# Attention in one kernel: the weights of a step are turned ahead of the next scores and copied ahead of the next exponential

## What is computed

```python
blocks = [(0, 16)] + [(s, min(s + 128, L)) for s in range(16, L, 128)]
for s, e in blocks:
    sc = einsum('bqhd,bkhd->bhqk', q[:, s:e], k[:, :e]) * 96 ** -0.5
    mask = arange(e)[None, :] <= arange(s, e)[:, None]
    p = softmax(where(mask, sc, -inf))
    outs.append(einsum('bhqk,bkhd->bqhd', p, v[:, :e]))
o = concatenate(outs, axis=1).reshape(bsz, L, 1024)
return o @ w_out
```

## Time and profile before

| | |
|---|---|
| median of 3 runs | 2978.79 us (2968.76 to 2986.44) |
| profiled execution | 2991.16 us, span 2989.3 |
| TensorE matmul busy | 2820.3 us, 94% of the span |
| TensorE weight load busy | 2387.6 us, 80% |
| VectorE, ScalarE, POOL busy | 1126.5, 1073.3, 968.6 us (38, 36, 32%) |
| mean granted TensorE clock | 0.942 |
| chain that ended last | PE 88%, DVE 6%, ACT 3%, issue 2% |
| HBM traffic | 211.24 MB read, 71 GB/s over the span |

### The profile page before, as it was taken

One profiled execution on the slowest core, in us unless ns is written; L12 is line 12 of the kernel. 1 busy time (PEld: TensorE's weight loads), 2 busy tenths in 40 slices (PEclk: granted clock), 3 DMA queues, 4 the chain that ended last, 5 costly groups with the idle time before them and its releaser, 6 DMA issues.

```text
span 2989.3 us, 38670 instructions
## 1 busy us (share of the span) xinstructions
PE 2820.3 (94%) x16552; PEld 2387.6 (80%) x16552; DVE 1126.5 (38%) x1571; ACT 1073.3 (36%) x1574; POOL 968.6 (32%) x413
## 2 busy tenths in 40 slices
PE   6999999799999978999999989999889999899999
PEld 4777778577777866777777989999857767699999
DVE  5333331433333166665555131112344344421111
ACT  3333332333333334544544232233343333333222
POOL 3343434334343431222222434443320000343442
PEclk9999999899999989999999999999986678899999
DMA  3232323123232211111111222222210000122222
GB/s 117 87 109 87 109 87 99 51 94 102 94 102 94 92 49 32 55 57 50 43 43 43 92 71 86 93 91 92 68 49 8 15 15 8 57 92 93 85 92 85
DMA packets 61289, 215.82 MB, mean 72 GB/s; under 512 B 8128, under 2 KB 8512, under 8 KB 61120
## 3 DMA queue, kind: packets, MB, share of 16 engines
q1 hardware_dynamic: 55440, 199.78, 20.3%
q10 hardware_dynamic: 5680, 13.58, 1.4%
HBM read 211.24 MB, written 2.10 MB: 71 GB/s over the span
## 4 chain that ended last, share of the span: by engine, by line
PE 88%; DVE 6%; ACT 3%; issue 2%; ACTq 0%; POOL 0%
PE psum L363 71%; PE psum L584 4%; PE psum L814 1%; PE psum L780 1%; PE psum L453 1%; PE psum L443 1%; PE psum L752 1%; PE psum L565 1%; DVE sb_square L1350 1%; PE psum L756 1%; PE psum L778 1%; PE psum L816 1%; DVE sb_scaled L1350 1%; PE psum L797 1%; PE psum L460 0%
## 5 line engine op out<-in xcount | busy, mean ns | idle before, releaser
L315 POOL TENSOR_TENSOR sb_w_lo<-sb_w_raw,sb_w_hi 128x1024 fp32r<-128x1024 f32 x377 | 916.3, 2434 | 1881.1 <-ACT sb_w_hi L941 1881.0
L363 PE MATMUL psum<-sb_h_hi,sb_w_hi 128*128 128x264 f32 (+1 forms) x2904 | 818.8, 334 | 65.7 <-DVE sb_h_lo L1354 51.3
L363 PE MATMUL psum<-sb_h_lo,sb_w_hi 128*128 128x264 f32 (+1 forms) x2904 | 800.1, 328 | 0.0
L363 PE MATMUL psum<-sb_h_hi,sb_w_lo 128*128 128x264 f32 (+1 forms) x2904 | 796.2, 326 | 0.0
L941 ACT ACTIVATE sb_w_hi<-sb_w_raw 128x1024 fp32r<-128x1024 f32 x377 | 395.1, 1053 | 567.4 <-PE psum L363 475.7
L363 PEld LDWEIGHTS psum<-sb_h_hi,sb_w_hi 128*128 128x128 f32 x2904 | 491.4, 190 | 129.9 <-issue 55.2
L363 PEld LDWEIGHTS psum<-sb_h_lo,sb_w_hi 128*128 128x128 f32 x2904 | 490.6, 190 | 47.2 <-issue 3.6
L363 PEld LDWEIGHTS psum<-sb_h_hi,sb_w_lo 128*128 128x128 f32 x2904 | 490.2, 191 | 44.9
L363 PE MATMUL psum<-sb_mix_hi,sb_w_hi 128*128 128x264 f32 (+1 forms) x1680 | 422.4, 315 | 6.9 <-DVE sb_mix_lo L1840 5.1
L363 PE MATMUL psum<-sb_mix_lo,sb_w_hi 128*128 128x264 f32 (+1 forms) x1680 | 420.2, 314 | 0.0
L363 PE MATMUL psum<-sb_mix_hi,sb_w_lo 128*128 128x264 f32 (+1 forms) x1680 | 418.8, 313 | 0.0
(11 more groups left out here) (235 smaller groups left out, 2643.3 us busy)
## 6 DMA issues: line engine op xcount, KB each, us to landing
sb_w_raw<-in_weights SPq DMA_DIRECT2D x377, 512.0 KB, 3.3
sb_decay<-in_decay ACTq DMA_DIRECT2D x16, 640.0 KB, 3.9
sb_resid<-in_x ACTq DMA_DIRECT2D x1, 2048.0 KB, 11.8
out<-sb_resid SPq DMA_DIRECT2D x8, 256.0 KB, 2.0
sb_table<-in_rope_table ACTq DMA_DIRECT2D x1, 264.0 KB, 2.6
sb_s<-in_positions ACTq DMA_DIRECT2D x1, 256.0 KB, 5.7
sb_cols<-in_cols ACTq DMA_DIRECT2D x1, 158.5 KB, 7.1
sb_resid<-in_meta ACTq DMA_DIRECT2D x1, 64.0 KB, 11.8
```

What stands on the lines that cost most here:

```text
L315: e.tensor_tensor(g.w_lo[:, u % 4, :], g.w_raw[:, u % 2, :], g.w_hi[:, u % 4, :].bitcast(F32), ALU.subtract).then_inc(S["w_lo"], 1)
L363: mm = e.matmul(g.psum[0:m, at + b, 0:wd], w[:, slot, P * i:P * i + m], xs[:, tile, c:c + wd], start=first and n == 0, stop=last and n == 2)
```

## The change

In each iteration of the loop, TensorE turns the weights of step i - 2 and multiplies those of step i - 3 by V ahead of the scores of step i; before, it turned those of i - 1 and multiplied those of i - 2 behind them. ScalarE copies the turned weights of step i - 2 ahead of the exponential of step i; before, it copied those of i - 1 behind it. The calls of `dve_finish` move from n = 1 and 5 to n = 2 and 6. Behind the loop stand the calls that the shift leaves over.

```diff
--- before.py
+++ after.py
@@ -873,11 +873,11 @@
     pe_pair_keys(g, e, 1)
     for i in range(ALL_STEPS):
         pair, n = divmod(i, NS)
+        if i >= 2:
+            pe_turn_p(g, e, i - 2)
+        if i >= 3:
+            pe_times_v(g, e, i - 3)
         pe_scores(g, e, i)
-        if i >= 1:
-            pe_turn_p(g, e, i - 1)
-        if i >= 2:
-            pe_times_v(g, e, i - 2)
         if pair + 1 < PAIRS:
             if n == 1:
                 pe_pair_totals(g, e, pair + 1, 0)
@@ -893,6 +893,8 @@
                 pe_pair_keys(g, e, pair + 2)
         for m, tiles in FILL.get(i, ()):
             pe_mla_out(g, e, m, tiles)
+    pe_turn_p(g, e, ALL_STEPS - 2)
+    pe_times_v(g, e, ALL_STEPS - 3)
     pe_turn_p(g, e, ALL_STEPS - 1)
     pe_times_v(g, e, ALL_STEPS - 2)
     pe_times_v(g, e, ALL_STEPS - 1)
@@ -1252,9 +1254,9 @@
     act_pair_keys(g, e, 1)
     for i in range(ALL_STEPS):
         pair, n = divmod(i, NS)
+        if i >= 2:
+            act_copy_pt(g, e, i - 2)
         act_exp(g, e, i)
-        if i:
-            act_copy_pt(g, e, i - 1)
         if pair and pair + 1 < PAIRS:
             if n == 0:
                 act_pair_keys(g, e, pair + 1)
@@ -1266,6 +1268,7 @@
             act_pair_out(g, e, pair - 1)
         if pair + 2 < PAIRS and n == 7:
             act_pair_q_squares(g, e, pair + 2)
+    act_copy_pt(g, e, ALL_STEPS - 2)
     act_copy_pt(g, e, ALL_STEPS - 1)
     act_pair_out(g, e, PAIRS - 1)
 
@@ -1854,9 +1857,9 @@
     for i in range(ALL_STEPS):
         pair, n = divmod(i, NS)
         dve_top(g, e, i)
-        if n == 1 and pair:
+        if n == 2 and pair:
             dve_finish(g, e, pair - 1, 1)
-        if n == 5:
+        if n == 6:
             dve_finish(g, e, pair, 0)
         if n == 6 and pair:
             dve_pair_out(g, e, pair - 1)
```

## The result

The changed kernel took 3024.80 us in the median of 4 runs (3024.39 to 3032.16), the kernel before 2980.34 beside it: a ratio of 1.0143, 95% interval 1.0122 to 1.0164. It is slower by 1.4%, 42.5 us. The forecast was 3009, its range 2986 to 3035. The profiled execution took 3024.94 (span 3023.1), 33.8 us more than that of before, for which the sum had said 30.1. That of before, 2991.16, is 11 us above its median, so the two profiles show less of a difference than the medians.

A forecast was written before the change was run, and what follows sets the result against it. TensorE's own stream was taken as the bound. Terms of 5.5, 0.1, 14.4 and 10.1 us, with 0 for the clock, sum to 30.1, giving 3009 us on the median 2978.8; own range 3000 to 3020, outer range 2986 to 3035.

The forecast's parts named there:

- a move of the extras: Extra work ending an iteration (totals, output turn, queries, keys; ScalarE's extras) goes ahead of turning and copy.
- n = 3 to 4: Scores of step n = 4 wait for a copy now behind both root halves: +2.05 us, 7 times, 14.4 us.
- n = 7 to 1: Scores of n = 0 wait for a copy behind query squares, 5.5 us; totals ahead of turning at n = 1, +0.1.
- rival A: Longer gaps keep the clock down, early returns in pairs 5 and 6 lost, falls come earlier: +54, 3033 us; chance 0.2.
- n = 6: Second queries wait for the previous output's low part, now also behind a finish on VectorE: 2.16 us idle, sum +10.1 us.
- The clock, taken as 0 net: Granted clock in the loop: later returns before n = 4 against earlier ones at n = 5, taken as 0 net.
- B: Denser blocks bring the clock's early return in pairs 0 to 4 too: -28, net +2, 2981 us; chance 0.11.
- C: Totals directly behind the scores of n = 1 keep the clock up: 38 us faster, 2941 us; chance 0.07.
- B2: The copy gets by the root, so no loss ahead of n = 4's scores: +16, 2995 us; chance 0.09.
- D: The change does what its words say and TensorE's listed waits go with nothing in exchange: 2960 us; chance 0.03.

The follow-up runs named there:

- experiment 1: Kernel before with only the TensorE and VectorE part of the change, ScalarE's order as before: 3006.3 us, ratio 1.0094.
- experiment 2: Kernel before with only ScalarE's new order, TensorE and VectorE as before: 3018.7 us, ratio 1.0126.
- Experiment 3: Changed kernel with ScalarE's copy at n = 3 put back ahead of the two halves of the reciprocal root: 3004.8 us, ratio 1.0085.
- experiment 9: Kernel of experiment 7; at n = 5 first queries ahead of turning and times V, exponential ahead of copy, finish behind last Newton step: 2962.1 us, ratio 0.9933.
- experiment 7: Kernel before with ScalarE's copy ahead of the exponential in every iteration and the keys at n = 7 instead of 6: 2970.2 us, ratio 0.9962.
- experiment 8: Changed kernel with the root at n = 3 and the squares at n = 7 back behind ScalarE's copy: 3015.4 us, ratio 1.0106.
- experiment 12: Kernel of experiment 8 with the output's low part on VectorE run at n = 5 instead of n = 6: 2967.6 us, ratio 0.9950.
- experiment 10: Kernel of experiment 7 with query squares ahead of copy and exponential at n = 7, and low part ahead of n = 6's maximum: 2946.3 us, ratio 0.9886.

## Why the prediction was right, and where its sizes were off

- **That the change is a move of the extras, not of the turning,** carried the direction. TensorE's and ScalarE's rows of the kernel after show it, and experiments 1 and 2 show each half to cost by itself.
- **n = 3 to 4:** forecast +14.4, measured +15.2 on that step, with 2.0 us ahead of the scores each time. Experiment 3 took it away alone, and the profiled loop lost 12 us with it. Shown.
- **n = 7 to 1:** forecast +5.6 over the steps 7-0, 0-1 and 1-2; measured +13.8. The squares cost their 0.9 us a time and the maximum came earlier, as worked out. But the gap of 0.9 to 1.0 us that was to stand ahead of the totals isn't there in pairs 1 to 6. In pair 3 the second product (2363.61 + 1.29) and the squared keys (2364.20 + 0.61) came when expected, and the scores of n = 1, which at the clock of before would have ended at about 2364.1, ended at 2365.57. The lower clock filled the gap with slower work. Over these steps idle time fell by 0.6 us and the busy time of the same work grew by 14.3: rival A's mechanism, which had been priced at 13.
- **n = 6:** the gap was forecast at 2.16 us and measured at 2.14 and 2.15, idle time over the steps 4-5 to 6-7 grew by 10.1 us, forecast 10.1. What these steps took in all is another matter, +4.5: -12.0 before n = 6, as the queries of n = 5 bring the clock back before the turning, worth more than the 0.8 us a pair written down (experiment 9 shows the same gain, 11 us, by itself), and +16.5 behind it, where in pairs 2 and 4 the clock falls in the middle of the queries.
- **The clock, taken as 0 net,** is the term that was mis-sized. In the two profiled loops the 34.8 us are 23 of idle time and 12 of busy time. The sum had 30.1 of idle time and none of busy time: it was 7 too high in the one, 6 of them the gaps ahead of the totals, and 12 too low in the other, and came within 4.7 us because these two errors cancel in part. That is luck. Against medians the change cost 44 us or, with the pooled runs of before (2982 to 2984), 41 to 43. So 11 to 14 us are left above the forecast's 30, and about 20 above the 23 of idle time; they are put down to the clock. The granted clock over the span was 0.935 to 0.937 in the four executions of the changed kernel and 0.940 to 0.949 in the 56 of before beside the experiments, which agrees; how much of the time it makes is argued from one trace of each kernel. The measured 3024.8 lies outside the forecast's own 3000 to 3020 and nearer to A's 3033 than to 3009; it is the outer range, which took in A, that holds it.
- **The rivals.** A held in large part: the earlier fall cost what it had said, and pairs 5 and 6 lost their early return (periods of 49.5 and 43.3 us, where 38.6 and 34.0 were). What it didn't have is the earlier return at n = 5. Nor can more gaps only lower the mean clock, as the prediction says there: experiment 1 has 20 us more of them than the kernel before and a mean of 0.71, not 0.70. B's early return before n = 4 did not come. C did not: the clock fell still earlier. B2 and D are out, as the gap of 2.0 us at n = 4 stands in seven pairs.
- Left open: which gap brings the clock down at a given time. Gaps of 1 us ahead of n = 0 didn't decide it (experiment 7). One of 2.1 us at n = 6 did (experiments 8 and 12: five falls with it, none without), but in the changed kernel the same gap stands in pairs 1 to 5 and only pairs 2 and 4 fall behind it, so it isn't enough by itself. Squares and root in front shifted the fall between n = 6 and 1 (experiments 3 and 8) in no order that I can derive.

## What to carry to other kernels

Work that is moved in a fixed stream is moved past everything between its old and its new place: write both orders of every engine down side by side, and price what waits for the piece that went back. Where the granted clock goes up and down, a gap on TensorE can cost twice, first its own length and then the work that follows at 1.2 GHz; so look for the gap whose removal keeps the upper level, which here was the place of one VectorE call. A sum of gaps that comes out near the measured time doesn't show that the gaps are the cause of all of it: compare idle and busy time apart. And an experiment that undoes parts of a loss can find a gain: the order of the change, with its two late inputs made early, beats the kernel before.

## What I had not expected of the hardware

- One gap of 2.14 us ahead of dense products, with 2.4 GHz before it, was followed within about 0.9 us of these products by 1.2 GHz, which held for 3.5 to 7 us in the middle of them, in five of eight pairs (experiment 8; pair 3 at 2396.6, the product that takes 0.52 us and then 0.63 instead of 0.40). Without the gap, the same stream stayed at 2.4 GHz for 20 us at a time (experiment 12).
- Kernels differ in spread, and the granted clock goes with it: experiment 7 stayed within 5.3 us in 10 runs (granted clock over the span 0.943 to 0.945), experiment 10 went over 26 in 4 (0.946 to 0.955), the kernel before over 22 in 25 (0.941 to 0.949).
